# A two-layer decoder step on one core: side matmuls cut into pieces between single products, and three V rows of a slot on the vector engine

## The chip, the cores and the metric

The kernel runs on one core of a Trainium2 chip. The metric is the device time of one execution in microseconds (us), the median of several. The core has TensorE (PE, matrix products into PSUM), VectorE (DVE), ScalarE (ACT), GpSimd (POOL) and SyncE (SP, which here issues plain transfers), and 16 DMA engines that serve the queues of all of them.

## The reference

One inference step of 576 tokens (512 of a prompt, 64 decoded) through two layers. Layer 0 mixes by a state-space model with a gated linear unit (GLU), layer 1 by windowed attention; each is followed by PEER, the retrieval of single experts, which is where nearly all the time goes:

```python
def one(xb):                                   # 128 tokens, D_MODEL = 1024
    q = (xb @ w_q).reshape(128, 8, 2, 128)     # 8 heads, two halves of a query
    s = einsum('bhcd,hcnd->bhcn', q, sub_keys) # against 2 x 128 keys
    sv, si = top_k(s, 16)
    cand = sv[:, :, 0, :, None] + sv[:, :, 1, None, :]
    fv, fi = top_k(cand, 16)                   # 16 experts of 16384 per token and head
    eid = ...                                  # their numbers
    g = softmax(fv)
    hpre = einsum('bd,bhkd->bhk', xb, u_tab[eid])
    a = gelu(hpre) * g
    return einsum('bhk,bhkd->bd', a, v_tab[eid])
```

All data is float32. A row of `u_tab` or `v_tab` is 4 KB, and each token, head and k reads its own row of both.

## The kernel before

The 576 tokens are five tiles: 0 to 3 have 128 tokens, tile 4 (`FULL`) has 64. The expert stage of a layer is 36 *slots*; a slot is one head of one tile, and for tile 4, which has half the rows, two heads packed into 128 rows. Slots are numbered 0 to 71 over both layers; the first 16 of a layer go over tiles 0 and 1, pair of heads by pair of heads (4 slots a pair), the other 20 over tiles 2, 3 and 4 (5 slots a pair, the fifth one packed). So 64 slots are unpacked and 8 are packed. A slot has 16 *positions* k, one for each chosen expert.

The engines are programmed by hand, each with its own ordered list, and meet by semaphores:

- POOL gathers for position k of slot j the U rows (`gather_u(j, k)`) and then the V rows of the slot before (`gather_v(j - 1, k)`), 128 rows of 4 KB each, into two rings of `RING` = 6 buffers. A U gather waits for the dot six positions earlier, a V gather for the consumer of the V row six positions earlier. A packed slot works alike.
- VectorE does at position k of slot j `dot(j, k)`, a product with row sum of the U rows and x, and then `between(j, k)`: a step of the selection for a later slot (`merge`, `name_experts`, `halves`), at k = 0 `weigh(j - 1)` (the coefficients `av` from Gelu and softmax) and, when a block of slots on the same tile is done, `flush(j - 2)`, which adds PSUM to H. In some slots it also mixes a GLU half (`MIX_IN`), or squares, refines and normalises a tile of x (`NORM_IN`).
- ACT makes for each V row a diagonal matrix of the coefficients (`DIAG`, four buffers), and has softmax, `gelu(j - 1)`, the copies out of PSUM, and the sigmoid of the GLU.
- TensorE multiplies each diagonal with its V row (two matmuls of 512 columns, `add_products`, L1449), accumulating in PSUM banks 0 and 1. Beside that it has side work: queries for a pair of heads some slots on (L1420, in the slots of `TURNED_IN`), scores (L1434), the GLU banks of tiles 2 to 4 (L1398, slots 2 to 9), and transposes of x (L1409, `NORM_IN`).

TensorE and ACT work through a slot in *quarters*: four products (or diagonals), then a whole block of side work. A block of queries or of one GLU bank is 8 matmuls. In TensorE's list a gate bank follows quarter 3, in ACT's list its sigmoid follows quarter 3 too, and the Gelu of the slot comes behind it. All 16 V rows of every slot go to TensorE: `DVE_ROWS = []`, so `add_row` is never called.

In the trace a float32 matmul is two records, so a product of one V row is four.

Of the kernel before, what the change touches and what calls it, by code (L numbers as in the profile page):

```python
# [22 lines left out]
P = 128  # L23
# [68 lines left out]
PE_ROWS = list(range(TOPK))  # L92
DVE_ROWS = []


class Slot:


    def __init__(self, layer, group, pair, tile, i):
# [4 lines left out]
        self.rows = list(range(TOPK)) if self.packed else PE_ROWS  # L104
# [35 lines left out]
def build(nc, io):  # L140
    with ExitStack() as ctx:
# [330 lines left out]
        def _(dve):  # L472
# [323 lines left out]
            def between(j, k):  # L796
# [17 lines left out]
                if at > 0 and k - 2 in DVE_ROWS and not SLOT[j - 1].packed:  # L814
                    add_row(j - 1, k - 2)
                if (j, k) in MIX_IN:
                    mix_half(MIX_IN[j, k])
                if j in NORM_IN:
                    if k == 5:
                        if NORM_IN[j] % TILES == FULL:  # L820
                            dve.wait_ge(twice, 16 * (NORM_IN[j] // TILES + 1))
                        dve.wait_ge(flushed, BLOCKS[j - 1])
                        mean_square(NORM_IN[j])
                    if k == 7:
                        refine(NORM_IN[j])
                    if k == 8:
# [3 lines left out]
                if j in FINAL_IN:  # L830
# [3 lines left out]
                    if k == 8:  # L834
# [202 lines left out]
        def _(act):  # L1037
# [95 lines left out]
            def diagonals(j, quarter):  # L1133

                rows = SLOT[j].rows
                n = len(rows) // 4
                if quarter == 0:
                    act.wait_ge(weights, j + 1)
                for i in range(quarter * n, quarter * n + n):
                    g = PE_DONE[j] + i  # L1140
                    if g > 3:
                        act.wait_ge(products, g - 3)
                    act.activation(DIAG[:, g % 4, :], (fold if SLOT[j].packed else ident)[:, :], ACT.Copy,  # L1143
                                   scale=av[:, j % 2, rows[i]:rows[i] + 1]).then_inc(diags, 1)

            def slot(j):

                at = j % PER_LAYER
                if at > 0:
                    gelu(j - 1)  # L1150
                    diagonals(j - 1, 0)
                if j == 1:
                    sc_copy(2)
                if at > 0:
                    diagonals(j - 1, 1)
                if 0 < j and at < PER_LAYER - 2:
                    sc_copy(j + 2)
                if j in NORM_IN:
                    root(NORM_IN[j])
                if j in FINAL_IN:  # L1160
                    final_root(FINAL_IN[j], P)
                if at > 0:
                    diagonals(j - 1, 2)
                if at < PER_LAYER - 1:
                    softmax(j + 1)
                if at > 0:
                    diagonals(j - 1, 3)
                if j == 0:
# [142 lines left out]
        def _(pe):  # L1311
# [462 lines left out]
```

## Time and profile before

| | us |
|---|---|
| median of 3 runs | 3941.02 |
| lowest, highest | 3939.73, 3950.24 |
| the profiled execution | 3943.76 |
| its span, first to last instruction | 3942.0 |

| engine | busy us | share |
|---|---|---|
| TensorE matmul | 3029.3 | 77% |
| VectorE | 2334.7 | 59% |
| POOL | 2391.4 | 61% |
| ScalarE | 890.8 | 23% |

The profile is one execution. Up to 320 us runs the state-space part, from 1932 to 2366 the attention, the rest are the slots. The software queue of the gathers (1208 MB of 1286) takes 78.5% of the 16 DMA engines over the span. The chain of work that ended last goes by TensorE (33%), DMA (27%) and POOL (22%). A busy share is a mean over stretches with different limits, so the table by stretch below says more than it.

### The profile page before, as it was taken

The numbers are of one execution on the slowest core, as the hardware profiler recorded it, in microseconds if no ns is written. First come the engines' busy times: TensorE is split into PE (matmuls) and PEld (weight loads), VectorE is DVE, ScalarE is ACT, GpSimd is POOL, SyncE is SP. The second block draws the span as 40 slices with busy tenths as digits, with TensorE's granted clock in tenths as the row PEclk, the third lists the DMA queues.
The fourth block names the chain that finished last, engine by engine and source line by source line (L and its number), as shares of the span: only waits on it lengthen the run. The fifth ranks groups of instructions, "written<-read, shape, count | busy, mean of one in ns | idle before, by whom it ended". The sixth has DMA issues, their size and how long they took to land.

```text
span 3942.0 us, 28375 instructions
## 1 busy us (share of the span) xinstructions
PE 3029.3 (77%) x8245; PEld 1375.6 (35%) x8245; DVE 2334.7 (59%) x5312; ACT 890.8 (23%) x2064; POOL 2391.4 (61%) x2313
## 2 busy tenths in 40 slices
PE   1477899988788787877787866787877787879776
PEld 1454344333333232422244443243333332424222
DVE  7936555566566666665334326666665666666663
ACT  2212222222122222222123211222222222222221
POOL 2005776777677777776500007777677777777774
PEclk9688999999999999999998978999999999999999
DMA  2457999999999999999800019999999999999997
GB/s 49 35 156 248 363 361 369 350 373 390 406 409 408 409 405 409 402 409 397 333 22 0 13 34 372 408 408 409 379 373 397 409 409 410 406 409 401 406 406 300
DMA packets 371977, 1286.47 MB, mean 326 GB/s; under 512 B 39708, under 2 KB 52508, under 8 KB 370716
## 3 DMA queue, kind: packets, MB, share of 16 engines
q0 software_dynamic: 331776, 1208.11, 78.5%
q1 hardware_dynamic: 40052, 76.59, 6.5%
q8 instruction: 68, 1.11, 0.1%
q14 instruction: 81, 0.66, 0.0%
HBM read 1280.18 MB, written 4.82 MB: 326 GB/s over the span
## 4 chain that ended last, share of the span: by engine, by line
PE 33%; DMA 27%; POOL 22%; issue 10%; DVE 5%; ACT 2%; SPq 1%; DVEq 0%; ACTq 0%; POOLq 0%
DMA arena<-in_peer_v,eid 23%; PE ps L1449 16%; POOL arena L1664 11%; POOL arena L1677 11%; PE ps L1420 5%; PE ps L1398 3%; DMA arena<-in_peer_u,eid 2%; PE ps L1505 2%; PE ps L1521 2%; DVE arena L476 1%; PE ps L1555 1%; PE ps L1533 1%; DVE arena L553 1%; SPq L390 1%; DMA arena<-kern 1%
## 5 line engine op out<-in xcount | busy, mean ns | idle before, releaser
L1449 PE MATMUL ps<-arena 128*128 128x512 f32 x4608 | 2215.7, 616 | 603.6 <-DMA arena<-in_peer_v,eid 466.8
L751 DVE CUSTOM_DVE_ANT_0 arena<-arena 128x1024 f32<-128x1024 f32 x1152 | 1410.4, 1225 | 1083.8 <-DMA arena<-in_peer_u,eid 1083.3
L1664 POOL DMA_INDIRECT arena<-in_peer_u,eid x1152 | 1172.2, 1018 | 917.9 <-DVE eid L741 564.7
L1449 PEld LDWEIGHTS ps<-arena 128*128 128x128 f32 x4608 | 827.8, 193 | 1917.4 <-issue 1220.2
L1677 POOL DMA_INDIRECT arena<-in_peer_v,eid x1152 | 1184.5, 1028 | 481.7 <-PE ps L1449 251.0
L1143 ACT ACTIVATE arena<-ident,av 128x128 f32<-128x128 f32 x1024 | 390.1, 399 | 1637.3 <-PE ps L1449 1498.2
L1420 PE MATMUL ps<-arena 128*128 128x320 f32 (+2 forms) x1088 | 263.4, 397 | 5.2 <-ACT arena L1102 3.3
L1420 PEld LDWEIGHTS ps<-arena 128*128 128x128 f32 x1088 | 200.4, 194 | 79.9 <-issue 29.4
L1398 PE MATMUL ps<-arena 128*128 128x512 f32 (+1 forms) x320 | 142.3, 601 | 5.2 <-DMA arena<-in_w_glu 5.2
L1505 PE MATMUL ps<-arena 128*128 128x512 f32 (+1 forms) x240 | 96.7, 563 | 13.6 <-ACT arena L1200 13.6
L1131 ACT ACTIVATE ge<-hp 128x16 f32<-128x16 f32 x72 | 15.5, 216 | 394.8 <-DVE hp L751 394.6
L751 DVE DVE_READ_ACCUMULATOR2_ANT hp<- 128x1 f32 x1152 | 94.6, 82 | 0.0
L1143 ACT ACTIVATE arena<-fold,av 128x128 f32<-128x128 f32 x128 | 49.0, 399 | 188.1 <-PE ps L1449 172.6
L1126 ACT ACT_TABLE_LOAD x71 | 91.1, 1283 | 1.2
L1131 ACT ACT_TABLE_LOAD x70 | 89.8, 1283 | 1.2
L1521 PE MATMUL ps<-arena 128*128 128x512 f32 (+1 forms) x160 | 79.1, 658 | 12.2 <-DVE arena L971 10.6
L1398 PEld LDWEIGHTS ps<-arena 128*128 128x128 f32 (+1 forms) x320 | 57.8, 182 | 86.6 <-issue 86.6
L781 DVE TENSOR_TENSOR arena<-arena,ps 128x1024 f32<-128x1024 f32 x40 | 48.6, 1214 | 58.9 <-PE ps L1449 58.9
L476 DVE TENSOR_TENSOR arena<-arena 128x512 f32<-128x512 f32 (+6 forms) x97 | 73.5, 777 | 2.5
L1505 PEld LDWEIGHTS ps<-arena 128*128 128x128 f32 x240 | 48.6, 206 | 58.3 <-issue 46.1
L760 DVE SCALAR_TENSOR_TENSOR av<-ge,sums,exps 128x16 f32<-128x16 f32 x72 | 16.7, 232 | 86.4 <-ACT ge L1131 86.4
L1363 PE MATMUL ps<-arena 128*72 128x128 f32 x128 | 18.0, 307 | 57.1 <-DMA arena<-kern 57.1
(198 smaller groups left out, 1749.9 us busy)
## 6 DMA issues: line engine op xcount, KB each, us to landing
arena<-in_peer_wq SPq DMA_DIRECT2D x16, 2048.0 KB, 18.7
arena<-in_peer_u,eid POOLq DMA_INDIRECT x1152, 10.4
arena<-in_peer_v,eid POOLq DMA_INDIRECT x1152, 10.5
arena<-in_w_glu SPq DMA_DIRECT2D x2, 4096.0 KB, 13.1
arena<-kern SPq DMA_DIRECT2D x8, 512.0 KB, 22.2
arena<-in_keys SPq DMA_DIRECT2D x16, 256.0 KB, 20.7
arena<-in_w_q SPq DMA_DIRECT2D x1, 4096.0 KB, 39.2
arena<-in_w_o SPq DMA_DIRECT2D x1, 4096.0 KB, 12.8
```

What stands on the lines that cost most here:

```text
L476: return dve.tensor_tensor(out, a, b, ALU.mult)
L751: dve.tensor_tensor_reduce(UROWS[:, g % RING, :], UROWS[:, g % RING, :], x_rows(SLOT[j].tile), 1.0, 0.0, ALU.mult, ALU.add, hp[:, j % 2, k ...
L1126: act.activation(exps[:, j % 2, :], best_v[:, :], ACT.Exp, bias=lowest[:, j % 2:j % 2 + 1], accum_out=sums[:, j % 2, 0:1]).then_inc(exps_d ...
L1131: act.activation(ge[:, j % 2, :], hp[:, j % 2, :], ACT.Gelu).then_inc(gelus, 1)
L1143: act.activation(DIAG[:, g % 4, :], (fold if SLOT[j].packed else ident)[:, :], ACT.Copy, scale=av[:, j % 2, rows[i]:rows[i] + 1]).then_inc ...
L1398: mm = pe.matmul(ps[0:n, bank, :], ZT[:, kt, t * P:t * P + n], WGLU[:, kt, at + 512 * b:at + 512 * (b + 1)], start=(kt == 0), stop=(kt == ...
L1420: mm = pe.matmul(ps[:, 3 + half, at], WQ[:, k, col:col + P], x[:, k, :], start=(k == 0), stop=(k == KT - 1))
L1449: mm = pe.matmul(ps[:, half, :], DIAG[:, (PE_DONE[j] + i) % 4, :], VROWS[:, g % RING, half * 512:(half + 1) * 512], start=(s.first and i = ...
L1505: mm = pe.matmul(out[:, b, :], xt[:, k, :], w[:, k, b * n:(b + 1) * n], start=(k == 0), stop=(k == KT - 1))
L1521: mm = pe.matmul(ps[0:n, 4 + b, :], OT[:, i, 0:n], WO[:, i, b * 512:(b + 1) * 512], start=(i == 0), stop=(i == QPK - 1))
L1664: pool.indirect_dma_start(UROWS[:, g % RING, :], None, tab_u, bass.IndirectOffsetOnAxis(ap=eid[:, j % 4, k:k + 1], axis=0))\
L1677: pool.indirect_dma_start(VROWS[:, g % RING, :], None, tab_v, bass.IndirectOffsetOnAxis(ap=eid[:, j % 4, k:k + 1], axis=0))\
```

## The change

The diff does four things.

1. `DVE_ROWS = (5, 9, 15)`: in an unpacked slot the V rows of positions 5, 9 and 15 are added to H by VectorE (`add_row`, one multiply-add of 128x1024), right behind the dot and the selection step of the same position of the next slot. ACT makes no diagonal and TensorE no product for them. POOL waits for `rows_added` before it fills their buffers again.
2. TensorE goes position by position: one product, then one piece of side work. Queries go two matmuls at each even position; a GLU bank one matmul at a time over `GLU_AT`, the 96 positions of slots 2 to 9 that the queries leave; transposes two at each of positions 9 to 12; scores at position 4.
3. ACT goes position by position too: `gelu` first, then diagonals, with the sigmoid at position 1 of the slot behind its bank, the copy of the queries at 2 of the next slot, the scores' copy at 6, softmax at 8, the copy of x at 15.
4. On VectorE the work in norm slots moves from positions 5, 7, 8 to 2, 5, 6, the mixes mostly from 13 to 10, and the final scale from 8 to 9.

```diff
-PE_ROWS = list(range(TOPK))
-DVE_ROWS = []
+DVE_ROWS = (5, 9, 15)
...
+COPIED_IN = {FIRST_USE[q] - 2: q for q in range(32) if q % 16 > 1}
+GLU_AT = [(j, k) for j in range(2, 10) for k in range(TOPK) if j not in TURNED_IN or k % 2]
+GLU_STEP = {at: n for n, at in enumerate(GLU_AT)}
+GATE_IN = {(3, 1): 0, (4, 1): 1, (5, 1): 2, (7, 1): 3, (8, 1): 4, (9, 1): 5}
+MIX_IN = {(3, 10): 0, (4, 10): 1, (6, 2): 2, (7, 10): 3, (8, 10): 4, (10, 1): 5}
...
-                if at > 0 and k - 2 in DVE_ROWS and not SLOT[j - 1].packed:
-                    add_row(j - 1, k - 2)
+                if at > 0 and k in SLOT[j - 1].dve_rows:
+                    add_row(j - 1, k)
...
+            def beside(j, k):                        # ACT
...
+                if k == 2 and j in COPIED_IN:
+                    q = COPIED_IN[j]
+                    turned_copy_of(q, slice(0, 2 * P + LAST * (q // 8 % 2)), q + 3)
...
+                if k == 6 and 0 < j and at < PER_LAYER - 2:
                     sc_copy(j + 2)
-                if j in NORM_IN:
+                if k == 8 and at < PER_LAYER - 1:
+                    softmax(j + 1)
+                if (j, k) in GATE_IN:
+                    sigmoid_half(GATE_IN[j, k])
+                if k == 3 and j in NORM_IN:
                     root(NORM_IN[j])
+                if k == 15 and j in NORM_IN:
+                    xt_copy(NORM_IN[j])
...
+            def beside(j, k):                        # TensorE
+
+                at = j % PER_LAYER
+                if j in TURNED_IN and k % 2 == 0:
                     q = TURNED_IN[j]
-                    if quarter == 0:
+                    if k == 0:
                         pe.wait_ge(xt_copied, 5 * (q // 16) + (5 if q // 8 % 2 else 2))
-                    queries(q, quarter, slice(0, 2 * P + LAST * (q // 8 % 2)), q + 2)
...
+                    first = k % 8
+                    queries(q, k // 8, slice(0, 2 * P + LAST * (q // 8 % 2)), q + 2, range(first, first + 2))
+                if k == 0 and j == 1:
+                    scores(2)
+                if k == 4 and 0 < j and at < PER_LAYER - 2:
                     scores(j + 2)
...
+                if (j, k) in GLU_STEP:
+                    n, kt = divmod(GLU_STEP[j, k], KT)
+                    n, value = divmod(n, 2)
+                    if kt == 0:
+                        pe.wait_ge(mixed if value else gated, n + 2)
+                    mm = gate_part(2 + n // 2, 6 if value else 5, n % 2, 0 if value else D, kt)
+                    if kt == KT - 1:
+                        mm.then_inc(value_ready if value else gate_mm, 1)
+                if j in NORM_IN and 9 <= k < 13:
+                    first = 2 * (k - 9)
+                    xt(NORM_IN[j], range(first, first + 2))
```

ACT's list from the second half of slot 6 to the start of slot 7, before: L1115 copies scores, L1122 and L1126 are softmax, L1084 the sigmoid, L1109 the copy of the queries, L1131 Gelu, L1143 diagonals.

```order
95 L1115 COPY arena<-ps 128x256
96 L1143 ACTIVATE arena<-ident,av 128x128 x4
97 L1122 ACTIVATE lowest<-best_v 128x1
98 L1126 ACT_TABLE_LOAD
99 L1126 ACTIVATE exps,sums<-best_v,lowest 128x16
100 L1143 ACTIVATE arena<-ident,av 128x128 x4
101 L1084 ACT_TABLE_LOAD
102 L1084 ACTIVATE arena<-ps 128x512
103 L1109 COPY arena<-ps 128x2x256
104 L1131 ACT_TABLE_LOAD
105 L1131 ACTIVATE ge<-hp 128x16
106 L1143 ACTIVATE arena<-ident,av 128x128 x8
```

The same place after the change, with the lines of the new kernel (L1086 sigmoid, L1133 Gelu, L1146 diagonals, L1111 the copy of the queries, L1117 of the scores):

```order
103 L1124 ACTIVATE lowest<-best_v 128x1
104 L1128 ACT_TABLE_LOAD
105 L1128 ACTIVATE exps,sums<-best_v,lowest 128x16
106 L1146 ACTIVATE arena<-ident,av 128x128 x5
107 L1133 ACT_TABLE_LOAD
108 L1133 ACTIVATE ge<-hp 128x16
109 L1146 ACTIVATE arena<-ident,av 128x128 x2
110 L1086 ACT_TABLE_LOAD
111 L1086 ACTIVATE arena<-ps 128x512
112 L1146 ACTIVATE arena<-ident,av 128x128
113 L1111 COPY arena<-ps 128x2x256
114 L1146 ACTIVATE arena<-ident,av 128x128 x3
```

The sigmoid and the copy of the queries now stand behind Gelu and the first diagonals of slot 7, where they stood in front of Gelu.

VectorE's list in a slot with a flush, from position 4 to position 7, before (L751 dot, L722 to L737 steps of the selection):

```order
713 L751 ISA arena,hp<-arena 128x1024
714 L751 ISA hp 128x1
715 L722 MAX_INDEX best_i<-best_v,arena 128x8
716 L751 ISA arena,hp<-arena 128x1024
717 L751 ISA hp 128x1
718 L729 TENSOR_SCALAR ab<-best_i 128x16
719 L730 TENSOR_SCALAR ab<-best_i 128x16
720 L751 ISA arena,hp<-arena 128x1024
721 L751 ISA hp 128x1
722 L732 TENSOR_TENSOR arena<-ab,iota 128x512
```

And after (L753 dot, L775 the added row):

```order
737 L753 ISA arena,hp<-arena 128x1024
738 L753 ISA hp 128x1
739 L724 MAX_INDEX best_i<-best_v,arena 128x8
740 L753 ISA arena,hp<-arena 128x1024
741 L753 ISA hp 128x1
742 L731 TENSOR_SCALAR ab<-best_i 128x16
743 L732 TENSOR_SCALAR ab<-best_i 128x16
744 L775 SCALAR_TENSOR_TENSOR arena<-arena,av 128x1024
745 L753 ISA arena,hp<-arena 128x1024
746 L753 ISA hp 128x1
```

The row of position 5 stands between its own dot, with the selection step of it, and the dot of position 6.

## Rows read from the trace of the kernel before

**Rows 1.** The page: a group (count, busy, mean ns, idle before), a DMA issue.

```profile
L1143 ACT ACTIVATE arena<-ident,av 128x128 f32<-128x128 f32 x1024 | 390.1, 399 | 1637.3 <-PE ps L1449 1498.2
...
arena<-in_peer_wq SPq DMA_DIRECT2D x16, 2048.0 KB, 18.7
```

**Rows 2.** Table by stretch: busy us of each engine (instructions), TensorE clock, DMA share, GB/s.

```profile
320.40:405.30 84.90, 57.72 (x196) 33.95 (x195) 57.42 (x141) 16.98 (x36) 58.09 (x50) 0.84 0.92 330
405.30:935.50 530.20, 458.21 (x1117) 206.17 (x1116) 312.19 (x759) 124.24 (x276) 386.31 (x355) 0.96 0.97 364
...
1079.60:1843.70 764.10, 610.86 (x1433) 247.79 (x1432) 489.93 (x1181) 176.82 (x420) 574.02 (x577) 1.00 1.03 408
...
2828.50:3014.50 186.00, 148.40 (x362) 66.31 (x362) 114.13 (x281) 46.92 (x104) 138.47 (x128) 0.95 0.97 368
3014.50:3894.80 880.30, 702.20 (x1626) 280.15 (x1624) 568.72 (x1347) 204.79 (x486) 662.39 (x668) 1.00 1.02 407
```

**Rows 3.** Waits, 405.3 to 935.5: us in total, times, longest.

```profile
ACT arena L1084 <- PE ps L1398: 86.7, 6, 20.9
DVE av L760 <- ACT ge L1131: 60.5, 8, 9.1
...
POOL arena L1677 <- PE ps L1449: 51.4, 51, 10.6
```

**Rows 4.** Timeline around 650 of TensorE, ACT, POOL: start, us, [idle before].

```profile
646.47 7.03 PE L1398 MATMUL ps<-arena 128*128 128x512 f32 x16
...
653.54 0.60 ACT L1084 ACTIVATE arena<-ps 128x512 f32<-128x512 f32 x1 [18.53 <-PE ps L1398]
...
661.65 1.58 POOL L1677 DMA_INDIRECT arena<-in_peer_v,eid  x1 [10.60 <-PE ps L1449]
```

**Rows 5.** Waits, 2828.5 to 3014.5.

```profile
ACT arena L1102 <- PE ps L1409: 44.0, 3, 18.4
...
POOL arena L1677 <- PE ps L1449: 14.0, 17, 7.1
```

**Rows 6.** Gathers by stretch, us to landing: 405.3 to 935.5, 1079.6 to 1843.7, 3648 to 3894.

```profile
arena<-in_peer_u,eid POOLq DMA_INDIRECT x178, 6.3
...
arena<-in_peer_u,eid POOLq DMA_INDIRECT x289, 11.7
...
arena<-in_peer_u,eid POOLq DMA_INDIRECT x93, 7.9
```

**Rows 7.** TensorE's timeline at 1172, a block of queries.

```profile
1172.30 4.47 PE L1420 MATMUL ps<-arena 128*128 128x320 f32 x16
```

**Rows 8.** Timeline from 1129, slot 17: TensorE, VectorE, POOL.

```profile
1129.60 1.96 PE L1449 MATMUL ps<-arena 128*128 128x512 f32 x4 [0.61 <-DMA arena<-in_peer_v,eid]
...
1133.32 1.22 DVE L751 CUSTOM_DVE_ANT_0 arena<-arena 128x1024 f32<-128x1024 f32 x1 [0.92 <-DMA arena<-in_peer_u,eid]
...
1134.47 0.17 DVE L729 TENSOR_SCALAR ab<-best_i 128x16 uint32<-128x16 uint32 x1
...
1133.10 0.94 POOL L1677 DMA_INDIRECT arena<-in_peer_v,eid  x1 [0.30 <-issue]
1134.35 1.01 POOL L1664 DMA_INDIRECT arena<-in_peer_u,eid  x1 [0.30 <-issue]
```

**Rows 9.** Timeline from 2853, a norm slot: VectorE's normalise, and POOL.

```profile
2853.45 1.28 DVE L658 SCALAR_TENSOR_TENSOR arena<-arena,rt 128x1024 f32<-128x1024 f32 x1
...
2854.06 1.48 POOL L1664 DMA_INDIRECT arena<-in_peer_u,eid  x1 [0.30 <-issue]
```

**Rows 10.** Timeline from 1121, a flush on VectorE, and POOL.

```profile
1121.82 1.21 DVE L781 TENSOR_TENSOR arena<-arena,ps 128x1024 f32<-128x1024 f32 x1
...
1122.86 0.94 POOL L1677 DMA_INDIRECT arena<-in_peer_v,eid  x1 [0.30 <-issue]
```

**Rows 11.** TensorE's timeline at 940, and the table by stretch of 938 to 944.

```profile
940.76 4.66 PE L1449 MATMUL ps<-arena 128*128 128x512 f32 x7 [3.15 <-DVE arena L781]
...
938.00:944.00 6.00, 3.24 (x5) 1.45 (x6) 4.66 (x11) 2.57 (x6) 4.78 (x5) 0.72 1.02 408
```

More of the change, by code:

```diff
@@ L1146, in slot, with diagonal @@
-            def slot(j):
+            def diagonal(j, k):
+                s = SLOT[j]
+                if k not in s.rows:
+                    return
+                i = s.rows.index(k)
+                g = PE_DONE[j] + i
+                if i == 0:
+                    act.wait_ge(weights, j + 1)
+                if g > 3:
+                    act.wait_ge(products, g - 3)
+                act.activation(DIAG[:, g % 4, :], (fold if s.packed else ident)[:, :], ACT.Copy,
+                               scale=av[:, j % 2, k:k + 1]).then_inc(diags, 1)
@@ L1161, in slot @@
+                if k == 7 and j in FINAL_IN:
                     final_root(FINAL_IN[j], P)
[L1162 to L1168, printed above, removed]
+                if k == 15 and j == 0:
                     root(1)
@@ L1186, in slots @@
                 for j in range(PER_LAYER * layer, PER_LAYER * (layer + 1)):
-                    slot(j)
+                    if j % PER_LAYER:
+                        gelu(j - 1)
+                    for k in range(TOPK):
+                        if j % PER_LAYER:
+                            diagonal(j - 1, k)
+                        beside(j, k)
                 end = PER_LAYER * (layer + 1)
                 gelu(end - 1)
-                for quarter in range(4):
-                    diagonals(end - 1, quarter)
+                for k in range(TOPK):
+                    diagonal(end - 1, k)
             def root_of(S, t):
@@ L1418, in queries @@
                 col = q % 2 * 2 * P + half * P
-                for k in range(KT):
+                for k in parts:
                     mm = pe.matmul(ps[:, 3 + half, at], WQ[:, k, col:col + P], x[:, k, :], start=(k == 0), stop=(k == KT - 1))
-                if half == 1:
+                if half == 1 and KT - 1 in parts:
                     mm.then_inc(turned_q, 1)
@@ L1454, in beside @@
-            def beside(j, quarter):
-                if j in TURNED_IN and quarter < 2:
+                pe.wait_ge(diags, PE_DONE[j] + i + 1)
+                pe.wait_ge(v_in[g % RING], 16 * (g // RING + 1))
+                for half in range(2):
+                    mm = pe.matmul(ps[:, half, :], DIAG[:, (PE_DONE[j] + i) % 4, :],
+                                   VROWS[:, g % RING, half * 512:(half + 1) * 512],
+                                   start=(s.first and i == 0), stop=False, skip_group_check=True)
@@ L1491, in att_project @@
+                for k in range(TOPK):
+                    add_product(PER_LAYER * (layer + 1) - 1, k)
             def att_project(S, t):
@@ L1621, in _ @@
                 for half in range(2):
-                    queries(q, half, columns(1), q + 2)
+                    queries(q, half, columns(1), q + 2, range(KT))
             slots(0)
@@ L1629, in _ @@
                 for half in range(2):
-                    queries(q, half, slice(0, 2 * P), q + 2)
+                    queries(q, half, slice(0, 2 * P), q + 2, range(KT))
             scores(PER_LAYER)
```

135 lines of the change are left out of this document (44 added, 91 removed).

## The prediction

> **What bounds the kernel now.** The work is 72 slots of 32 gathers each. A gather is 128 rows of 4 KB, 0.524 MB, so a slot moves 16.8 MB. I read first the table by stretch [rows 2], cut where a slot's first dot starts. From 1079.6 to 1843.7 (slots 16 to 33) the core moves 408 GB/s with a DMA share of 1.03: there the transfers are the bound, 41.1 us per slot at 408 GB/s, and a faster engine is worth nothing. From 405.3 to 935.5 (slots 2 to 12) it is 364 GB/s, in the layer's first stretch 330, from 2828.5 to 3014.5 (slots 47 to 50) 368. Time lost against 408 GB/s is the length times (1 - rate/408): 16.2 us in the first stretch, 57.2 in slots 2 to 12, 18.2 in slots 47 to 50, 92 us in all. Outside these little can be won.
>
> Who starves the queue there? In slots 2 to 12 [rows 3] POOL waits 51.4 us for products of TensorE before V gathers, once 10.6 us. DVE's weigh waits 60.5 us for ACT's Gelu, in 8 waits up to 9.1, and ACT waits 86.7 us for L1398, the GLU matmuls, in 6 waits. The timeline from 640 shows one such chain [rows 4]: TensorE runs a whole GLU bank (16 records, 7.03 us) from 646.5, ACT's sigmoid stands in front of Gelu and has waited 18.53 us when it starts at 653.54, Gelu, weigh and the first product follow, and POOL's next V gather at 661.65, 10.60 us late. In slots 47 to 50 [rows 5] it is the same with another blocker: ACT waits 44.0 us for L1409, the transposes of x behind the last products of a slot, and POOL loses 14.0 us, 7.1 of them at once.
>
> How much of a stall the DMA feels depends on what is queued. A U gather lands 11.7 us after its issue in slots 16 to 33 and 6.3 us in slots 2 to 12 [rows 6]; in the last slots 7.9 us go with the full rate (407 GB/s from 3014.5, [rows 2]). So between 11.7 and about 7 there is a reserve that stalls may eat, and at 6.3 each one is paid. The stalls in slots 16 to 33, behind blocks of query matmuls of 4.47 us [rows 7], cost only reserve.
>
> **The change, part by part.** (1) *ACT is no longer blocked.* The sigmoid moves from the end of a slot (behind the last diagonal, in front of the next Gelu) to position 1 of the next slot; the last piece of its bank was issued one position before that slot began. The xt copy waits at position 15 for transposes issued at 9 to 12. So the waits of 86.7 and 44.0 us go, and with them nearly all of POOL's 51.4 and 14.0 us. What is late next is POOL itself: without waits it issues at its own pace. In slots 2 to 12 that is 386.3 us for 355 issues [rows 2], 1.09 each, plus 0.30 between two [rows 8]: 1.39 x 32 = 44.4 us per slot, 3.3 more than the transfers need. This pace holds only while there is no reserve; the first load of the next query weights (2048 KB, [rows 1], 5.1 us of the queue) builds one. I leave 3 such slots in the first stretch (slot 2, which comes before that load, and two of the three with norm work), 10 us of the 57.2, and one in layer 1, 4 of the 18.2. Gain 47 + 14 = 61 us.
>
> (2) *TensorE's work per slot.* Four records of a product take 1.96 us by the timeline, and 16 in a row 7.03, so 0.44 each and 1.76 per row of V. A slot with a gate bank and a value bank holds 16 x 1.76 + 2 x 7.03 = 42.2 us, more than the 41.1 of the transfers; with 13 rows it is 36.9. Cutting side work into pieces adds no matmul; a product waits at most for one piece (0.88 us for one GLU matmul of two records, 1.1 for two queries, from 4.47/16 x 4) where it waited 7.03 or 4.47. Off the path as soon as ACT isn't late, so I count nothing for it beyond (1), except that the reserve is no longer spent at [rows 7].
>
> (3) *Three rows on VectorE.* There are 64 unpacked slots, so 192 rows leave TensorE (192 x 1.76 = 338 us of work) and ACT (192 x 0.399 = 77 us, [rows 1]), and 192 instructions reach VectorE. The nearest row is normalise, also 128x1024 from two SBUF tensors: 1.28 us [rows 9]. 192 x 1.28 = 246 us. In the full-rate stretch VectorE is busy 489.9 of 764.1 us; 15 unpacked slots add 15 x 3 x 1.28 = 58 us, so 64% becomes 72%. None of it is on the path if it fits between two dots, which are 2.56 us apart (two gathers of 0.524 MB at 408 GB/s = 2.57). At position 5: dot starts at 0, the two small instructions behind it at 1.15 and 1.23 (1134.47 against 1133.32 for the first of the two, [rows 8]), the row at 1.30, after its V row landed (one gather behind the U row, 1.28). It ends at 2.58, the next dot is due at 2.56, and the next position has less than 2.56 us of work on VectorE, so 0.02 is made up there. Positions 9 and 15 have less in front. Cost 0 in the full-rate stretch. On POOL's side there is a hold: an issue that starts while a two-tensor instruction of VectorE runs ends 0.81 us after that instruction's end (2854.06 + 1.48 = 2855.54 against 2854.73), where a free issue takes 0.94 [rows 9]. The flush, which reads one operand from PSUM, holds nothing: the issue at 1122.86 inside it takes 0.94 [rows 10]. In the steady pattern [rows 8] issues start 0.22 before a dot and 1.03 after it, the second is held a little (1.01), and the third would start at 2.34: the added row holds it by 2.58 - 2.34 = 0.24, it ends at 3.39 instead of 3.28, the fourth starts at 3.70, inside the next dot, which has to end anyway (2.56 + 1.22 + 0.81 = 4.59) and ends where it would have. So the hold is swallowed: between 0 (this) and 1.24 us, a whole lost issue, per row, I take 0. Where there is no reserve (slots 1, 2 and 37) I charge 9 rows x 0.24 = 2 us.
>
> (4) *VectorE's norm work earlier, mixes earlier.* Position 5 of a norm slot gets the root refinement and a row, 6 normalise (1.28). Some 1.5 us late for two positions, against U gathers issued 11.7 us ahead; nothing counted beyond the slots left in (1). The wait for the V row is the one new wait on VectorE: the next dot, and weigh and flush behind it, stand behind it, and POOL's U gather of six positions on waits for that dot. A V gather issued late would so delay U gathers too; with stalls gone I count 0.
>
> Sum: -61 + 2 = -59 us. The profiled run took 3943.8 us (span 3942.0 and 1.8 around it), 2.7 above the median of 3941.0; 3943.8 - 59 = 3884.8, and on the median's scale **3882 us**. Its own range is 3862 (all 75 us of slots 2 to 12 and 47 to 50 won, and 4 of the 16 in the first stretch) to 3905 (36 us won, so about half of the 75 kept).
>
> **Rivals.** (a) *Slower: the shared reads cost whole issues.* The steady pattern has no spare place for POOL: 0.94 + 0.30 = 1.24 against 1.28 per gather. If an added row pushes an issue behind the next dot, a whole issue of 1.24 us is lost and comes back only with the weights' loads (5.1 us per pair of heads, 1.3 per slot). It speaks for this that issues in slots 2 to 12 average 1.09 us instead of 0.94. Against it: the hold worked out above is 0.24 us and ends before the next dot. It bites from about one lost issue per slot; near two (64 x (1.8 x 1.24 - 1.3) = 60) the gain of 59 us is gone, and beyond that the kernel is slower than before. If all three are lost: 64 x (3 x 1.24 - 1.3) = 155 us, 155 - 59 = +96, 4037 us; if 2.2 are, some 3970. The Trainium skill has this rule ("GPSIMD Engine Reference", Key points): GpSimd shares its SBUF interfaces with VectorE and contends with instructions that have two SBUF inputs. The trace agrees by the issue of 1.48 us and by the flush that held none; applied at full length to each added row it would give up to 246 us more and no gain, which is this rival, so it gets its own chance.
>
> (b) *Half the gain: TensorE's clock.* Behind a position without a product TensorE idles 2 x 2.56 - 1.96 = 3.2 us. After an idle time of 3.15 us at 940.76 the granted clock of 938 to 944 was 0.72, so part of it at 1.2 GHz instead of 2.4 [rows 11]; in the full-rate stretch, where idle times are 0.61 us [rows 8], it was 1.00. At 1.2 GHz a product takes 3.5 us, over the 2.56 of a position; V rows come free late, up to 1.3 us per such stretch, and reserve is eaten. Against it: each 1.28 us of reserve lost gives the next V gather as much more slack, so it stops by itself. With that, or with the sigmoid and its table load at position 1, between diagonals 1 and 2, leaving a stall, 30 of the 61 us: 3913.
>
> (c) *No change: the stall only moves.* A GLU piece now waits for the mix or sigmoid with products behind it, and VectorE waits for V rows with dots behind it. One such wait of 6 us in each of the 14 slots 2 to 12 and 47 to 49 would cost 84 us of stall for the 65 removed. What TensorE's pieces wait for was issued at least six positions earlier (the mix at 10 for a piece at 0, the sigmoid at 1 for a piece at 8), so I give it little: 3941.
>
> **How the numbers follow.** Forecast (3862 to 3905) 0.60; (b) 0.14; (c) 0.08; (a) 0.18. A measurement of this kernel can tell 0.3%, 12 us, from no change: faster below 3929. Faster 0.60 + 0.14 = 0.74, within 0.08, slower 0.18. Below 3855 there is next to nothing; from 3855 to 3948 lie the forecast, (b) and most of (c), 0.81 together.
>
> **What the new profile would show.** Right: 405 to 900 at 400 GB/s or more; POOL's wait for L1453 in slots 2 to 12 under 12 us; no weigh waiting over 3 us for Gelu there; landing near 11 us; the added row 1.28 us, VectorE's busy time up by about 246 and TensorE's down by over 300; slots 16 to 33 still 408 GB/s. (a) shows as a rate under 400 GB/s in slots 16 to 33 with POOL busy all the time and landing near 6; (b) as a clock under 0.9 there; (c) as long waits of TensorE's L1396 or of the added row. Wrong would be the forecast if slots that now run at 408 GB/s lose any of it.

## The result: 0.7% slower

The changed kernel takes 3978.4 us (median of 8 runs, 3955.9 to 3986.9) against 3946.5 us of the kernel before (8 runs, 3939.7 to 3954.1). The ratio is 1.0072, 95% interval 1.0049 to 1.0095. The forecast of 3882 us was wrong. The time lies outside its own range (3862 to 3905) and outside the wide one of 3855 to 3948.

The page of the profile after, engines' busy us with their share and count of instructions, and the span in 40 slices (granted TensorE clock, DMA, GB/s):

```profile
span 3979.0 us, 27025 instructions
...
PE 2860.7 (72%) x7477; PEld 1321.4 (33%) x7477; DVE 2573.1 (65%) x5504; ACT 797.2 (20%) x1872; POOL 2507.0 (63%) x2313
...
PEclk9688999988888988898899968898889989899988
DMA  1456999999999999999700039999999999999997
GB/s 49 36 153 236 370 378 391 398 401 384 405 406 396 384 390 405 377 409 403 272 0 1 12 116 369 409 406 409 387 367 403 401 396 409 392 409 387 372 356 290
...
L1678 POOL DMA_INDIRECT arena<-in_peer_v,eid x1152 | 1248.3, 1084 | 392.4 <-issue 278.7
...
L775 DVE SCALAR_TENSOR_TENSOR arena<-arena,av 128x1024 f32<-128x1024 f32 x192 | 246.5, 1284 | 29.9 <-DMA arena<-in_peer_v,eid 20.4
...
arena<-in_peer_u,eid POOLq DMA_INDIRECT x1152, 7.7
```

The added rows are what was worked out: 192 of them, 1.28 us each, 246.5 us. What was not is the last line: over the whole program a U gather lands 7.7 us after its issue (median), where before it was 10.4, so the queue holds less. The table by stretch of the kernel after shows where (us; busy us of PE, PEld, DVE, ACT and POOL; clock; DMA share; GB/s). The stretches are slots 0 and 1, 2 to 12, 16 to 33, 47 to 50, and 51 to 71, as in [rows 2], and slots 65 to 70 by themselves:

```profile
320.50:412.60 92.10, 54.40 (x184) 32.31 (x182) 60.66 (x143) 14.89 (x32) 57.40 (x50) 0.81 0.85 304
412.60:908.60 496.00, 414.58 (x992) 180.30 (x992) 355.72 (x794) 110.53 (x247) 388.06 (x355) 0.95 1.01 389
1058.30:1840.80 782.50, 578.61 (x1252) 243.13 (x1252) 544.76 (x1226) 154.57 (x375) 605.62 (x573) 0.90 1.02 397
2827.40:3010.00 182.60, 136.82 (x304) 61.15 (x304) 129.54 (x294) 37.96 (x88) 143.57 (x129) 0.88 1.00 381
3010.00:3932.50 922.50, 662.81 (x1412) 270.53 (x1412) 635.20 (x1404) 179.74 (x434) 716.64 (x674) 0.91 1.01 392
3615.60:3889.60 274.00, 188.41 (x380) 73.58 (x380) 180.28 (x395) 51.51 (x124) 215.46 (x193) 0.91 0.98 368
```

Slots 2 to 12 are 34 us shorter than before (496.0 against 530.2), as meant. But slots 16 to 33, which ran at 408 GB/s, now run at 397 and are 18 us longer, and slots 51 to 71 are 42 us longer. Slots 0 and 1 are 7 us longer. In slots 65 to 70, where no weights are loaded any more, it is 45.7 us a slot, and POOL is busy 215.5 us for 193 issues, 1.12 each, with 0.30 between: POOL issues as fast as it can. The same six slots before:

```profile
3607.50:3855.10 247.60, 195.52 (x441) 75.11 (x440) 161.61 (x379) 58.08 (x138) 188.77 (x192) 1.00 1.02 405
```

They took 26 us less, with 0.98 us per issue.

The stalls of [rows 3] did go. Waits of the kernel after in slots 2 to 12 (us in total, times, longest):

```profile
DVE arena L753 <- DMA arena<-in_peer_u,eid: 131.5, 131, 2.6
...
ACT ge L1133 <- DVE hp L753: 79.4, 11, 10.9
...
POOL arena L1678 <- PE ps L1453: 6.4, 21, 0.3
```

POOL's 51.4 us of waiting for products is 6.4, at 0.3 each the usual step between two issues; Gelu now waits for the last dot, and weigh no longer for Gelu. So the loss comes from something else, in slots all over the program.

### The profile page after: what moved, and what is told of

It is laid out like the page before. It is cut to its first block, busy times and chain, and to the rows that moved or that the text cites. A ratio compares the mean times of both kernels' runs of the same rounds, so it can differ in the third digit from the quotient of the medians.

```text
span 3979.0 us, 27025 instructions
## 1 busy us (share of the span) xinstructions
PE 2860.7 (72%) x7477; PEld 1321.4 (33%) x7477; DVE 2573.1 (65%) x5504; ACT 797.2 (20%) x1872; POOL 2507.0 (63%) x2313
## 4 chain that ended last, share of the span: by engine, by line
POOL 32%; PE 25%; DMA 21%; issue 13%; DVE 6%; ACT 2%; SPq 1%; DVEq 0%; ACTq 0%; POOLq 0%
DMA arena<-in_peer_v,eid 19%; POOL arena L1665 16%; POOL arena L1678 16%; PE ps L1453 13%; PE ps L1424 2%; PE ps L1506 2%; PE ps L1522 2%; PE ps L1396 2%; DVE arena L478 1%; DVE arena L775 1%; PE ps L1556 1%; DVE arena L555 1%; PE ps L1534 1%; DMA arena<-in_peer_u,eid 1%; SPq L392 1%
## 5 line engine op out<-in xcount | busy, mean ns | idle before, releaser
L1453 PE MATMUL ps<-arena 128*128 128x512 f32 x3840 | 2036.7, 667 | 813.9 <-DMA arena<-in_peer_v,eid 560.5
L753 DVE CUSTOM_DVE_ANT_0 arena<-arena 128x1024 f32<-128x1024 f32 x1152 | 1410.3, 1224 | 918.7 <-DMA arena<-in_peer_u,eid 917.4
L1665 POOL DMA_INDIRECT arena<-in_peer_u,eid x1152 | 1224.2, 1063 | 928.8 <-DVE eid L743 564.6
L1678 POOL DMA_INDIRECT arena<-in_peer_v,eid x1152 | 1248.3, 1084 | 392.4 <-issue 278.7
L1453 PEld LDWEIGHTS ps<-arena 128*128 128x128 f32 x3840 | 750.7, 209 | 1924.1 <-issue 1433.4
L1146 ACT ACTIVATE arena<-ident,av 128x128 f32<-128x128 f32 x832 | 306.5, 396 | 1191.0 <-PE ps L1453 1022.9
L1424 PE MATMUL ps<-arena 128*128 128x320 f32 (+2 forms) x1088 | 318.3, 426 | 12.8 <-issue 7.5
L1424 PEld LDWEIGHTS ps<-arena 128*128 128x128 f32 x1088 | 220.2, 213 | 175.9 <-issue 145.8
L775 DVE SCALAR_TENSOR_TENSOR arena<-arena,av 128x1024 f32<-128x1024 f32 x192 | 246.5, 1284 | 29.9 <-DMA arena<-in_peer_v,eid 20.4
L1396 PE MATMUL ps<-arena 128*128 128x512 f32 (+1 forms) x320 | 157.5, 613 | 5.0 <-DMA arena<-in_w_glu 5.0
L1133 ACT ACTIVATE ge<-hp 128x16 f32<-128x16 f32 x72 | 15.5, 216 | 591.8 <-DVE hp L753 591.8
L1117 ACT COPY arena<-ps 128x256 f32<-128x256 f32 x72 | 26.8, 372 | 530.8 <-PE ps L1438 526.9
L1506 PE MATMUL ps<-arena 128*128 128x512 f32 (+1 forms) x240 | 96.6, 563 | 13.6 <-ACT arena L1199 13.6
L753 DVE DVE_READ_ACCUMULATOR2_ANT hp<- 128x1 f32 x1152 | 95.3, 83 | 0.0
L1522 PE MATMUL ps<-arena 128*128 128x512 f32 (+1 forms) x160 | 79.1, 658 | 12.2 <-DVE arena L973 10.6
L1146 ACT ACTIVATE arena<-fold,av 128x128 f32<-128x128 f32 x128 | 48.0, 397 | 168.0 <-PE ps L1453 150.1
L1506 PEld LDWEIGHTS ps<-arena 128*128 128x128 f32 x240 | 48.5, 206 | 58.2 <-issue 46.0
```

The source lines that it names most:

```text
L753: dve.tensor_tensor_reduce(UROWS[:, g % RING, :], UROWS[:, g % RING, :], x_rows(SLOT[j].tile), 1.0, 0.0, ALU.mult, ALU.add, hp[:, j % 2, k ...
L775: dve.scalar_tensor_tensor(H[:, t, :], VROWS[:, g % RING, :], av[:, j % 2, k:k + 1], H[:, t, :], ALU.mult, ALU.add).then_inc(rows_added, 1)
L1133: act.activation(ge[:, j % 2, :], hp[:, j % 2, :], ACT.Gelu).then_inc(gelus, 1)
L1146: act.activation(DIAG[:, g % 4, :], (fold if s.packed else ident)[:, :], ACT.Copy, scale=av[:, j % 2, k:k + 1]).then_inc(diags, 1)
L1396: return pe.matmul(ps[0:n, bank, :], ZT[:, kt, t * P:t * P + n], WGLU[:, kt, at + 512 * b:at + 512 * (b + 1)], start=(kt == 0), stop=(kt = ...
L1424: mm = pe.matmul(ps[:, 3 + half, at], WQ[:, k, col:col + P], x[:, k, :], start=(k == 0), stop=(k == KT - 1))
```

## Where an issue is lost

The timeline of slot 17 of the kernel after, positions 5 to 8, VectorE and then POOL (start, us, the line, idle time before and what ended it):

```profile
1112.24 1.23 DVE L753 CUSTOM_DVE_ANT_0 arena<-arena 128x1024 f32<-128x1024 f32 x1 [0.93 <-DMA arena<-in_peer_u,eid]
...
1113.62 1.28 DVE L775 SCALAR_TENSOR_TENSOR arena<-arena,av 128x1024 f32<-128x1024 f32 x1
1114.82 1.22 DVE L753 CUSTOM_DVE_ANT_0 arena<-arena 128x1024 f32<-128x1024 f32 x1
...
1115.96 0.69 DVE L734 TENSOR_TENSOR arena<-ab,iota 128x512 f32<-128x512 uint32 x1
1117.36 1.23 DVE L753 CUSTOM_DVE_ANT_0 arena<-arena 128x1024 f32<-128x1024 f32 x1 [0.71 <-DMA arena<-in_peer_u,eid]
...
1119.91 1.23 DVE L753 CUSTOM_DVE_ANT_0 arena<-arena 128x1024 f32<-128x1024 f32 x1 [0.71 <-DMA arena<-in_peer_u,eid]
...
1112.01 0.93 POOL L1678 DMA_INDIRECT arena<-in_peer_v,eid  x1 [0.30 <-PE ps L1453]
1113.25 1.03 POOL L1665 DMA_INDIRECT arena<-in_peer_u,eid  x1 [0.30 <-issue]
1114.58 1.13 POOL L1678 DMA_INDIRECT arena<-in_peer_v,eid  x1 [0.30 <-issue]
1116.02 1.44 POOL L1665 DMA_INDIRECT arena<-in_peer_u,eid  x1 [0.30 <-issue]
1117.76 1.63 POOL L1678 DMA_INDIRECT arena<-in_peer_v,eid  x1 [0.30 <-issue]
1119.70 0.94 POOL L1665 DMA_INDIRECT arena<-in_peer_u,eid  x1 [0.30 <-issue]
```

Read POOL's rows against VectorE's. The issue at 1114.58 meets the added row and ends 0.81 us after it (1113.62 + 1.28 = 1114.90), as foreseen. The next one starts at 1116.02, when the dot of position 6 has 0.02 us to run. It does not get through: the selection step L734, which also reads two tensors from SBUF, has been running since 1115.96 (in the trace it overlaps the end of the dot by 0.08 us), and the issue ends 0.81 us after that one (1116.65). Now POOL is late enough to start its next issue, at 1117.76, in the middle of the dot of position 7, and is held in the same way (to 1119.39, 0.80 us past the dot's end). At 1119.70 it stands again 0.21 us before a dot, the usual place. In the three dots from 1112.24 to 1119.91 it has made five issues and not six. One gather of reserve, 1.28 us of the queue, is gone.

Slot 17 is no special case. I counted, over the whole trace, the issues that start at the very end of the dot of position 6 and are held by L734 behind it: 42 in the 64 unpacked slots of the changed kernel, none in the kernel before.

That is theory T. The rivals that the experiments should tell apart: R1, each row on VectorE costs about the same; R2, TensorE is the cause, by its pieces or by its clock, which fell from 0.95 to 0.89 (rival (b) of the prediction).

## The experiments

All start from the changed kernel. Ratios are to the kernel before on the same chip. The runs were made on several chips, where the kernel before had medians of 3942.6 to 3949.8, so a difference of a few us between two lines is better read from the ratios.

| kernel | us | ratio (95%) | clock | landing, slots 16 to 33 |
|---|---|---|---|---|
| no row on VectorE | 3894.9 | 0.9871 (0.9850 to 0.9891) | 0.956 | 11.8 |
| row 9 | 3900.1 | 0.9884 (0.9862 to 0.9907) | 0.938 | 10.4 |
| row 5 | 3942.6 | 1.0000 (0.9979 to 1.0021) | 0.944 | 10.2 |
| rows 9, 15 | 3903.3 | 0.9883 (0.9856 to 0.9911) | 0.914 | 9.2 |
| rows 3, 9, 15 | 3931.7 | 0.9962 (0.9948 to 0.9977) | 0.899 | 9.2 |
| rows 5, 9, 15 (the change) | 3978.4 | 1.0072 (1.0049 to 1.0095) | 0.893 | 7.9 |
| row 9, then a two-tensor instruction | 3949.3 | 0.9993 (0.9970 to 1.0016) | 0.938 | 10.4 |
| row 9, then a one-tensor instruction | 3902.7 | 0.9874 (0.9844 to 0.9903) | 0.940 | 11.7 |
| row 5, selection steps one later | 3910.6 | 0.9909 (0.9887 to 0.9932) | 0.943 | 10.4 |
| pieces, row 9 in slots 2 to 8, slot 1 mended | 3887.8 | 0.9846 (0.9814 to 0.9877) | 0.956 | 11.7 |

The second table shows where the time goes: us between the first dots of the slots, in the profiled execution of each kernel. "Hold" is what POOL's issues of slots 65 to 70 take beyond 0.94 us each, per slot. "Edge" counts the issues of the whole trace that the two-tensor step (L734, or the inserted one) behind a dot holds, as L734 did at 1116.02.

| kernel | slots 2 to 12 | 16 to 33 | 47 to 50 | 65 to 70 | hold | edge |
|---|---|---|---|---|---|---|
| the kernel before | 530.2 | 764.1 | 186.0 | 247.6 | 1.5 | 0 |
| no row on VectorE | 486.4 | 764.8 | 171.9 | 248.1 | 1.5 | 0 |
| row 9 | 486.3 | 765.7 | 171.1 | 248.0 | 1.5 | 0 |
| row 5 | 497.3 | 764.8 | 186.4 | 264.6 | 4.3 | 50 |
| rows 9, 15 | 478.7 | 766.4 | 173.1 | 251.3 | 2.3 | 2 |
| rows 3, 9, 15 | 501.0 | 765.3 | 179.8 | 261.0 | 4.3 | 2 |
| rows 5, 9, 15 (the change) | 495.9 | 782.5 | 182.6 | 274.0 | 5.8 | 42 |
| row 9, then a two-tensor instruction | 493.9 | 762.3 | 185.5 | 264.4 | 4.6 | 57 |
| row 9, then a one-tensor instruction | 488.3 | 765.2 | 172.4 | 247.9 | 1.5 | 2 |
| row 5, selection steps one later | 486.5 | 765.5 | 179.8 | 248.0 | 1.5 | 10 |

### No row on VectorE

```diff
-DVE_ROWS = (5, 9, 15)
+DVE_ROWS = ()
```

> The changed kernel with all 16 rows of every slot on TensorE (DVE_ROWS empty): side work in pieces, ACT by positions, earlier norm work, nothing added on VectorE. Theory T (the loss is the row of position 5: it shifts POOL so that its issue meets the two-tensor selection step of position 6, and one issue of 1.24 us per slot is lost): the reserve of the queue stays over 8 us in slots 16 to 33, 408 GB/s there, time 3895 +- 12 (61 us won, some 7 lost in slot 1 where the queries now stand in front of the second product). Rival R1 (each added row costs the same): also 3895. Rival R2 (pieces on TensorE and its lower clock free the V rows late): stays at 3970.

3894.9 us. The pieces and the new order of ACT are worth 1.3% by themselves; R2 falls as far as it blames the pieces. The table by stretch, slots 1, 2 to 12, 16 to 33, 47 to 50:

```profile
352.40:414.60 62.20, 48.18 (x167) 29.64 (x168) 28.68 (x84) 12.84 (x29) 34.90 (x33) 0.88 0.81 293
414.60:900.90 486.30, 451.41 (x1125) 196.84 (x1124) 314.45 (x759) 124.64 (x280) 373.85 (x353) 0.99 1.02 397
1045.80:1810.70 764.90, 614.49 (x1433) 247.91 (x1432) 489.93 (x1181) 173.19 (x420) 574.76 (x578) 0.99 1.03 408
2794.40:2966.30 171.90, 142.94 (x352) 61.88 (x351) 114.70 (x280) 42.75 (x100) 133.19 (x128) 0.99 1.02 402
```

Slots 2 to 12 run at 397 GB/s and 16 to 33 at 408. Slots 2 to 12 are 44 us shorter than before, where the prediction's first step had 47. Slots 47 to 50 are 14 us shorter, as forecast, but slots 51 to 64 are 7 us longer (600.4 against 593.0): the load of query weights that is issued in slot 50 landed in slot 50 before and lands in slot 51 now. Slots 38 to 64 together are 9 us shorter. Slot 1 alone is 62.2 us; more of that below.

### One row: position 5 or position 9

```diff
-DVE_ROWS = (5, 9, 15)
+DVE_ROWS = (5,)
```

> Only the row of position 5 on VectorE. T: one issue lost per unpacked slot as with three rows, landing falls to 6 to 8 us, time 3965 +- 15. R1: a third of the loss of the three rows, 3923. R2: 3972.

```diff
-DVE_ROWS = (5, 9, 15)
+DVE_ROWS = (9,)
```

> Only the row of position 9 on VectorE; the selection step behind the next dot has one input tensor. T: nothing lost, as with no row, 3895 +- 12, landing over 10 us in slots 16 to 33. R1: 3923, as with the row at 5. R2: 3972.

The row of position 5 costs 47.7 us over no row, that of position 9 costs 5.2. Both are 64 instructions of 1.28 us and both take one product from TensorE. R1 falls, and R2's clock with it: 0.944 and 0.938. The 5.2 us of row 9 are within the noise.

For row 5 I had expected 3965 +- 15 by T and got 3942.6. The sign and the gap are T's; the size is 48 us over no row, two thirds of the 70 I had said. The reserve did not go as I said either. I had expected landing to fall to 6 to 8 us; in slots 16 to 33 it is 10.2, hardly below the 10.4 of row 9, and these slots lose no time (764.8 us). The time is lost where the reserve is small: slots 65 to 70 take 16.5 us more and a gather lands there in 6.4 us, against 10.4 without the row. That is 2.8 us a slot, more than the one issue of 1.24 us that T has. POOL's holds account for it (4.3 us a slot, against 1.5). Of the 2.8 us more, 0.7 fall to the row and to L734 and 2.0 to the dots: an issue that has lost its place just before a dot starts inside the dot and is held until 0.81 us after its end.

### The row of 3 in place of 5, and no third row

```diff
-DVE_ROWS = (5, 9, 15)
+DVE_ROWS = (3, 9, 15)
```

> Three rows as in the changed kernel, but at 3, 9 and 15 instead of 5, 9 and 15; behind the dots of positions 4 and 10 stand one-tensor steps. T: 3900 +- 15, 408 GB/s in slots 16 to 33 and 51 to 64. R1: 3978, as the changed kernel. R2: 3975; and its clock stays near 0.89 whatever the time.

```diff
-DVE_ROWS = (5, 9, 15)
+DVE_ROWS = (9, 15)
```

> Rows 9 and 15 on VectorE, none at 5 or 3. Measured so far: no row 3894.9 us, row 9 alone 3900.1, row 5 alone 3942.6, rows 3, 9, 15 3931.7, rows 5, 9, 15 3978.4. If row 15 is free (its next position's weigh is 0.23 us, the flush reads PSUM), 3903 +- 8. If row 15 is the one that costs in the two sets of three, 3930.

Rows 9 and 15 together cost 8 us by the medians and 5 by the ratios, within the noise, so two rows in three can be had nearly free. Row 3 on top costs 28 us, row 5 on top 75. For rows 3, 9 and 15 I had expected 3900 +- 15 by T and got 3931.7, so T misses here. A third row is dear at both places I tried, and at 5 it is worst. Slots 16 to 33 ran at 406 GB/s both with and without row 3 and with the same 9.2 us to landing; the time goes in slots 2 to 12, 47 to 50 and 65 to 70. It is POOL's holds again (4.3 us a slot in slots 65 to 70, against 2.3), but not T's edge, which is met twice and not 42 times. How row 3 makes them stays open; I have no experiment on it. The clock is 0.914 with rows 9 and 15 at 3903 us and 0.899 with 3, 9 and 15 at 3932, so a low clock alone does not set the time.

### The step behind the next dot

This is the test of T by itself: make the harmless row 9 harmful by an instruction behind the dot of position 10, once with two tensors from SBUF, once with one, of equal length (0.68 us). The added results are not used.

```diff
-DVE_ROWS = (5, 9, 15)
+DVE_ROWS = (9,)
...
+                if k == 10 and at > 1 and not SLOT[j - 1].packed:
+                    route.settle()
+                    route(dve.tensor_tensor(EQ, EQ, EQ, ALU.add))
```

> Row 9 alone, plus an extra tensor_tensor of 128x512 from SBUF twice right behind the dot of position 10 in slots that follow an unpacked one (its result is not used). It is the instruction that stands behind the dot of position 6. Theory T: this makes row 9 as dear as row 5, one issue lost per slot: 3940 +- 12, landing down to 6 to 8 us. Rival (any 0.7 us more on VectorE does nothing, the price of row 5 is its place in the slot): 3900.

```diff
-                    route(dve.tensor_tensor(EQ, EQ, EQ, ALU.add))
+                    route(dve.tensor_reduce(CAND[:, 0:2, :], EQ, AX.X, ALU.add))
```

> The same as the kernel with the extra two-tensor instruction, but with an extra tensor_reduce of 0.68 us that reads one SBUF tensor. T: no hold on POOL, 3901 +- 8. Rival (it is VectorE's time behind the row, not the second read): as the two-tensor one, about 3940.

3949.3 against 3902.7 us: 46.6 us apart, on one chip. The two instructions differ in the second input and also in what they write, 512 columns or 32. The write alone is not it: the reads from PSUM in the flush write 1024 columns to SBUF, and of the 440 issues in all traces that start while VectorE adds a tensor from PSUM to one from SBUF, none took over 0.95 us. The timeline of the two-tensor kernel, slot 17 from the row of position 9 on:

```profile
1126.96 1.28 DVE L775 SCALAR_TENSOR_TENSOR arena<-arena,av 128x1024 f32<-128x1024 f32 x1
1128.16 1.22 DVE L753 CUSTOM_DVE_ANT_0 arena<-arena 128x1024 f32<-128x1024 f32 x1
...
1129.31 0.68 DVE L807 TENSOR_TENSOR arena<-arena 128x512 f32<-128x512 f32 x1
...
1127.91 1.14 POOL L1668 DMA_INDIRECT arena<-in_peer_u,eid  x1 [0.31 <-issue]
1129.36 1.44 POOL L1681 DMA_INDIRECT arena<-in_peer_v,eid  x1 [0.30 <-issue]
1131.11 1.62 POOL L1668 DMA_INDIRECT arena<-in_peer_u,eid  x1 [0.30 <-issue]
1133.03 0.94 POOL L1681 DMA_INDIRECT arena<-in_peer_v,eid  x1 [0.30 <-issue]
```

And the same place of the one-tensor kernel:

```profile
1120.43 1.28 DVE L775 SCALAR_TENSOR_TENSOR arena<-arena,av 128x1024 f32<-128x1024 f32 x1
1121.64 1.22 DVE L753 CUSTOM_DVE_ANT_0 arena<-arena 128x1024 f32<-128x1024 f32 x1
1122.78 0.68 DVE L807 TENSOR_REDUCE arena<-arena 128x32 f32<-128x512 f32 x1
...
1121.37 1.16 POOL L1681 DMA_INDIRECT arena<-in_peer_v,eid  x1 [0.30 <-issue]
1122.83 0.94 POOL L1668 DMA_INDIRECT arena<-in_peer_u,eid  x1 [0.30 <-issue]
1124.08 0.94 POOL L1681 DMA_INDIRECT arena<-in_peer_v,eid  x1 [0.30 <-issue]
```

The first held issue is alike (1.14 and 1.16). The second starts 0.02 and 0.03 us before the dot's end in both; in the first kernel it takes 1.44 and the third 1.62, within 0.01 of those of the changed kernel; in the second kernel both take 0.94. Over the whole trace the inserted two-tensor instruction holds an issue in this way 56 times, the one-tensor instruction never.

That T's mechanism is there is shown, and so is its price at this place. Not shown is T's account by reserve. Landing in slots 16 to 33 was to fall to 6 to 8 us and is 10.4, and these slots lose nothing; the time goes, as with row 5, in slots 2 to 12, 47 to 50 and 65 to 70, and some of it in slots 36 to 46.

### The row of 5, with the step moved

```diff
-DVE_ROWS = (5, 9, 15)
+DVE_ROWS = (5,)
...
-                    if at < PER_LAYER - 1 and 5 <= k < 10:
-                        name_experts(j + 1, k - 5)
+                    if at < PER_LAYER - 1 and 6 <= k < 11:
+                        name_experts(j + 1, k - 6)
```

> Only the row of position 5 on VectorE, as in the run that took 3942.6 us, but the five selection steps of positions 5 to 9 each one position later (6 to 10), so that two small one-tensor instructions stand behind the dot of position 6 and the two-tensor step behind that of position 7. Theory T (it is the two-tensor step behind the dot that follows the row): 3900 +- 10, landing over 10 us in slots 16 to 33. Rival (the row at position 5 costs whatever stands behind it): 3942.

3910.6 us, at the edge of what T gave: of the 48 us that row 5 costs, 32 are back by the medians, 36 by the ratios. Slots 65 to 70 take 248.0 us, as without a row. Slot 17 of this kernel, with two small one-tensor steps behind the dot of position 6:

```profile
1104.96 1.28 DVE L775 SCALAR_TENSOR_TENSOR arena<-arena,av 128x1024 f32<-128x1024 f32 x1
1106.16 1.22 DVE L753 CUSTOM_DVE_ANT_0 arena<-arena 128x1024 f32<-128x1024 f32 x1
1107.30 0.17 DVE L731 TENSOR_SCALAR ab<-best_i 128x16 uint32<-128x16 uint32 x1
...
1105.92 1.14 POOL L1678 DMA_INDIRECT arena<-in_peer_v,eid  x1 [0.30 <-issue]
1107.36 0.94 POOL L1665 DMA_INDIRECT arena<-in_peer_u,eid  x1 [0.30 <-issue]
1108.60 0.94 POOL L1678 DMA_INDIRECT arena<-in_peer_v,eid  x1 [0.30 <-issue]
```

The remaining 16 us over no row are not in slots 16 to 33 (407 GB/s); the stretch of slots 47 to 50 has 385 GB/s where it had 402 without a row, and is 8 us longer. There norm work stands in the same positions. The two-tensor step at position 7 still holds an issue at a dot's end 10 times. I did not follow either further.

### The queries of slot 1, and a kernel that beats both

In slot 1 of the changed kernel TensorE does one product and then stands (its timeline):

```profile
364.84 1.98 PE L1453 MATMUL ps<-arena 128*128 128x512 f32 x4 [2.69 <-ACT arena L1146]
374.36 2.05 PE L1424 MATMUL ps<-arena 128*128 128x256 f32 x4 [7.53 <-issue]
```

The first piece of the queries waits there for the load of its weights and keys, the last of which landed at 374.27, and the second product stands behind it; before, four products came first. The last kernel puts these queries at positions 4 to 11 of slot 1. It has no row on VectorE but that of position 9 of slots 2 to 8, where TensorE has the GLU.

```diff
-DVE_ROWS = (5, 9, 15)
+DVE_ROWS = ()
...
+for s in SLOT[2:9]:
+    s.dve_rows = (9,)
+    s.rows = [k for k in range(TOPK) if k != 9]
...
-                if j in TURNED_IN and k % 2 == 0:
+                if j in TURNED_IN and (4 <= k < 12 if j == 1 else k % 2 == 0):
                     q = TURNED_IN[j]
-                    if k == 0:
+                    n = k - 4 if j == 1 else k // 2
+                    if n == 0:
                         pe.wait_ge(xt_copied, 5 * (q // 16) + (5 if q // 8 % 2 else 2))
-                    first = k % 8
-                    queries(q, k // 8, slice(0, 2 * P + LAST * (q // 8 % 2)), q + 2, range(first, first + 2))
+                    first = 2 * (n % 4)
+                    queries(q, n // 4, slice(0, 2 * P + LAST * (q // 8 % 2)), q + 2, range(first, first + 2))
```

> Side work in pieces, no row on VectorE except the row of position 9 of slots 2 to 8, where TensorE has GLU work, and in slot 1 the queries at positions 4 to 11 instead of 0 to 14, so that the second product does not stand behind the load of their weights. T: 3894.9 - 7 (slot 1) - 6 (slots 9 and 10) = 3882 +- 8. If slot 1's loss is not the queries' wait: 3889.

3887.8 us, 1.5% faster than the kernel before. Its slot 1:

```profile
347.50:399.70 52.20, 45.58 (x167) 28.40 (x168) 28.61 (x84) 12.74 (x29) 34.93 (x32) 0.94 0.96 348
```

52.2 us against 62.2 without the shift (54.6 before the change), so the queries' wait was slot 1's loss; this rests on the profiles. The time by itself does not tell: 3887.8 is in T's range and nearer to the 3889 of the rival. Of the 13 us expected over no row the medians show 7, with intervals that overlap.

## Why the prediction was wrong

**Step 1, ACT is no longer blocked: right.** The waits went as named and the kernel without rows is 51 us faster than before on its chip (0.9871 of 3945.7), where the sum had 61. Slots 2 to 12 gave 44 of the 47 us. Layer 1 gave 9 of the 14 us (slots 38 to 64 together), and slot 1 cost 7.5 us that the prediction did not have.

**Step 2, TensorE's pieces: right but for slot 1.** Rival (c) named a piece that waits with products behind it, and I gave it little because what the GLU pieces wait for was issued long before. I looked at GLU pieces alone; the one that did wait was a query piece, for a load. 7.5 us at one place.

**Step 3, the rows on VectorE: this is the step that failed.** It put the cost of the three rows at 2 us; they cost 79 by the ratios (0.9871 to 1.0072), 84 by the medians. Duration (1.28), hold (0.81 us behind the two-tensor instruction's end) and count were right. The working took 0 to 1.24 us per row and chose 0, on the ground that the fourth issue starts inside the next dot "and ends where it would have". Two things were wrong in that. The row starts 1.38 to 1.40 us after its dot and not 1.30, so the fourth issue falls at the dot's end to within 0.03 us. And I checked it against the dot alone. At position 6 a two-tensor step follows the dot; at 10 a one-tensor step, and at 0 weigh, 0.23 us. The cost was therefore near 0 at 9 and 15, and at 5 a whole issue (1.24 us), the upper end of my own bounds; where there is little reserve it was more, 2.8 us a slot for row 5 in slots 65 to 70.

**Rival (a) is what happened**, at 18%, with its sign: 397 GB/s in slots 16 to 33, under the 400 it named. Its threshold, that a slot can lose about one issue before it loses time because the weights' loads give it back, held in slots 16 to 33: row 5 alone adds 1.0 us of hold to a slot there and costs no time, the three rows add 2.0 us and cost 1.0 us a slot. It did not hold as an average over the program, since slots 65 to 70 have no loads and pay in full. So 3978 next to the "some 3970" of 2.2 lost issues per slot is partly luck. Row 5 alone costs 48 us, together with rows 9 and 15 it costs 75. That rows which are cheap alone leave less to spare for row 5 fits, but is argued, not shown. The Trainium skill's rule on GpSimd and VectorE ("GPSIMD Engine Reference", Key points) says that the two contend when a VectorE instruction has two SBUF inputs. It bears on this as a condition and not as a price. The traces agree with it by the holds (1.44 and 1.63 us), but by its words all three rows are alike, and the runs show at most 8 us for rows 9 and 15 together and 48 to 75 for row 5.

**Rival (b), the clock**: the clock did fall (0.953 to 0.893), with more rows the more, as the idle time of 3.2 us suggested. I found no price for it: rows 9 and 15 have 0.914 and cost 8 us, row 5 has 0.944 and costs 48.

**Reserve as the currency** was right in kind: the losses sit where landing is short. But I took "about 7 us" as safe, and a median hides what is under it. Slots 16 to 33 of the changed kernel have 7.9 us, as the last slots had before at the full rate, and lose 18 us: between slices at 410 GB/s lie some at 360 to 370. The rate in 40 slices of slots 16 to 33, then the landing there and in slots 65 to 70:

```profile
GB/s 410 410 408 410 409 403 395 370 393 407 408 406 409 410 366 367 369 362 389 378 405 409 410 409 410 395 402 396 372 360 361 392 409 410 409 410 409 409 410 408
...
arena<-in_peer_u,eid POOLq DMA_INDIRECT x287, 7.9
...
arena<-in_peer_u,eid POOLq DMA_INDIRECT x96, 6.1
```

## What to carry to other kernels

When POOL issues gathers at nearly the pace at which they are moved, place a two-tensor instruction on VectorE by where POOL's issues stand against it and against everything up to the second instruction after it; a row of 1.28 us cost 0.1 us at one place and 0.75 at another. Write such a pattern out to the hundredth from the trace, and where an issue falls within a tenth of a microsecond of an edge, take the worse side for the sum. A change with a scheduling part and a moved-work part should be split before it is judged: one part here was worth 1.3% and the other cost 2%.

## What the runs showed of the hardware

- An issue of a gather that starts while VectorE runs an instruction on two SBUF tensors ends 0.81 us after it, if that is later than the 0.94 us of a free issue. So it was, within 0.04 us, for all 207 issues of the changed kernel that started inside a 128x1024 multiply-add.
- One that starts at the very end of such an instruction is held by the next two-tensor instruction, if that has begun (1.44 us, in the changed kernel and in the test). Over all traces there are 271 issues that start while a dot ends and a two-tensor step behind it has begun; the 226 of them with at most 0.035 us of the dot left were held by the step, the 45 with 0.038 us or more were not.
- An instruction that reads one SBUF tensor (the inserted one), or one and PSUM (the flush, 0.95 us at most), held none.
- Holds do not simply add up: in slot 17 a shift of POOL's issue by 0.1 to 0.2 us was swallowed where no two-tensor instruction followed the next dot, and cost a whole issue of 1.24 us where one did. In time that was nothing in slots 16 to 33, where the queue has a reserve, and 2.8 us a slot in slots 65 to 70.
